# Interleaving the high and low activation halves, and moving four sums of squares from GpSimd to VectorE

## The reference

```python
def rmsnorm(x, g):                       # ahead of every layer
    return x * rsqrt(mean(x * x, axis=-1) + EPS) * g

x = x + rglru(rmsnorm(x, a_norm_g))      # norm 0
kv = rmsnorm(x, kv_norm_g) @ w_kv        # norm 1 (the attention layer uses the same root)
x = x + swa(rmsnorm(x, b_norm_g), kv)    # norm 1, second gain
x = x + 0.5 * swiglu(rms_norm(x, ffn1_norm))       # norm 2
x = x + hybrid_mixer(rms_norm(x, mix_norm))        # norm 3
x = x + 0.5 * swiglu(rms_norm(x, ffn2_norm))       # norm 4
return rms_norm(x, final_norm)                     # norm 5
# swiglu(x) = (silu(x @ w_gate) * (x @ w_up)) @ w_down, d_ff = 2816
```

## Time and profile before

| | us |
|---|---|
| Median of three runs (825.06 to 826.43) | 826.13 |
| The profiled execution | 825.43 |
| Its span, first to last instruction | 823.3 |
| TensorE busy | 799.1 |
| VectorE busy | 576.3 |
| ScalarE busy | 488.9 |
| GpSimd busy | 125.4 |

### The profile page before, as it was taken

How to read it: one execution, slowest core, us unless ns; L and a number is a source line. 1 busy time by engine, 2 the same in 40 slices (tenths; PEclk the granted TensorE clock), 3 DMA queues, 4 the chain that set the end, 5 groups by cost and what they waited for, 6 DMA issues and landing times.

```text
span 823.3 us, 15019 instructions
## 1 busy us (share of the span) xinstructions
PE 799.1 (97%) x5557; PEld 730.7 (89%) x5557; DVE 576.3 (70%) x840; ACT 488.9 (59%) x764; POOL 125.4 (15%) x172
## 2 busy tenths in 40 slices
PE   8999899799899999999999999999999999999997
PEld 7999899798699888889998889998999888888885
DVE  5987978777669787777448755466587788777443
ACT  7679855667756665555346455665747565555343
POOL 9305600325704000000003003000001200000000
PEclk9999999999999999999999999999999999999999
DMA  8624466443326676665655544444545576665661
GB/s 268 208 78 128 132 214 194 146 138 101 103 79 198 196 218 182 181 199 159 217 183 147 189 153 130 153 129 128 180 140 178 172 228 182 192 185 181 198 185 52
DMA packets 101046, 136.31 MB, mean 166 GB/s; under 512 B 5065, under 2 KB 86401, under 8 KB 100993
## 3 DMA queue, kind: packets, MB, share of 16 engines
q1 hardware_dynamic: 99232, 133.23, 52.4%
q0 software_dynamic: 1600, 2.28, 1.0%
q10 hardware_dynamic: 160, 0.07, 0.0%
HBM read 134.51 MB, written 1.05 MB: 165 GB/s over the span
## 4 chain that ended last, share of the span: by engine, by line
PE 73%; DVE 3%; ACT 2%; POOL 1%; issue 1%; ACTq 0%; DVEq 0%; POOLq 0%
PE bank L528 25%; PE bank L597 17%; PE bank L594 10%; PE bank L641 7%; PE bank L536 6%; PE bank L592 2%; PE bank L825 1%; PE bank L845 1%; DVE w_lo L1534 1%; ACT arena L1055 1%; POOL arena L474 1%; PE bank L838 1%; ACT w_hi L1055 1%; DVE arena L1856 1%; PE bank L1018 1%
## 5 line engine op out<-in xcount | busy, mean ns | idle before, releaser
L1534 DVE TENSOR_TENSOR w_lo<-stage,w_hi 128x1024 fp32r<-128x1024 f32 x249 | 318.3, 1285 | 149.2 <-ACT w_hi L1055 148.7
L528 PE MATMUL bank<-acts,w_hi 128*128 128x256 f32 (+1 forms) x1936 | 355.0, 285 | 5.4 <-DVE w_lo L1534 2.6
L1055 ACT ACTIVATE w_hi<-stage 128x1024 fp32r<-128x1024 f32 (+1 forms) x251 | 261.5, 1049 | 98.9 <-PE bank L528 53.2
L528 PEld LDWEIGHTS bank<-acts,w_hi 128*128 128x128 f32 x1936 | 302.4, 192 | 10.1 <-issue 6.0
L528 PE MATMUL bank<-acts,w_lo 128*128 128x256 f32 (+1 forms) x968 | 274.5, 284 | 0.0
L597 PE MATMUL bank<-acts,w_hi 128*128 128x512 f32 x616 | 217.5, 396 | 0.0
L594 PE MATMUL bank<-acts,w_lo 128*128 128x256 f32 x704 | 189.7, 280 | 0.0
L528 PEld LDWEIGHTS bank<-acts,w_lo 128*128 128x128 f32 x968 | 186.2, 192 | 0.0
L597 PEld LDWEIGHTS bank<-acts,w_hi 128*128 128x128 f32 x616 | 115.7, 188 | 25.5
L594 PEld LDWEIGHTS bank<-acts,w_lo 128*128 128x128 f32 x704 | 132.7, 188 | 3.6
L1055 ACT ACTIVATE arena<-bank 128x512 f32<-128x512 f32 (+1 forms) x79 | 44.1, 558 | 69.9 <-PE bank L597 46.5
(11 more groups left out here) (187 smaller groups left out, 711.0 us busy)
## 6 DMA issues: line engine op xcount, KB each, us to landing
stage<-ffn_w_gate SPq DMA_DIRECT2D x44, 512.0 KB, 4.2
stage<-ffn_w_up SPq DMA_DIRECT2D x44, 512.0 KB, 4.4
stage<-ffn_w_down SPq DMA_DIRECT2D x44, 512.0 KB, 4.0
stage<-w_in SPq DMA_DIRECT2D x40, 512.0 KB, 3.6
stage<-a_w_in SPq DMA_DIRECT2D x24, 512.0 KB, 4.7
stage<-b_w_in SPq DMA_DIRECT2D x16, 512.0 KB, 3.6
stage<-a_w_out SPq DMA_DIRECT2D x12, 512.0 KB, 4.0
stage<-b_w_out SPq DMA_DIRECT2D x8, 512.0 KB, 3.5
```

What stands on the lines that cost most here:

```text
L528: mm = pe.matmul(dst, w[:, slot, c:c + P], a[:, k, :] if isinstance(k, int) else wide(a[:, bass.ds(k, 1), :]), start=start and n == 0, sto ...
L1055: return nc.scalar.activation(out_, in_, func, **kw)
L1534: dve.tensor_tensor(w_lo[:, n % RING, 0:w], src, w_hi[:, n % RING, 0:w].bitcast(F32), ALU.subtract)\
```

## The change

The tensor `acts` gets another order: for each tile, high and low halves lie beside one another, so that `acts[:, k, :, :]` is one run of 512 columns, where before it was two runs of 256 that lie 30 tiles apart. Instructions that write several tiles of `a_hi` or `a_lo` at once now write runs of 256 with a gap of 256 between them, where before they wrote one run. No instruction is added or dropped for that.

All four calls of `square_sums` leave GpSimd's program. VectorE does the sums at the end of `norm`, in three instructions of 1024, 512 and 256 columns, each waiting for the one ahead of it.

```diff
+POOL_SUMS = []
+DVE_SUMS = [1, 2, 3, 4]
...
-        acts = sb("acts", [P, 2, 30, T], F32R)
-        a_hi, a_lo = acts[:, 0, :, :], acts[:, 1, :, :]
+        acts = sb("acts", [P, 30, 2, T], F32R)
+        a_hi, a_lo = acts[:, :, 0, :], acts[:, :, 1, :]
...
+        def each(t2):
+            return t2.rearrange("p (t n) -> p t n", n=T)
...
-            square_sums(1)
...
-            square_sums(2)
             pool.dma_start(fin_gain[:, :], I["final_norm_2"].rearrange("(o d) -> o d", o=1).to_broadcast([P, D]))\
                 .then_inc(fin_gain_in, 16)
-            square_sums(3)
             for h in range(NH):
                 normalise(NQ + h)
-            square_sums(4)
...
-                            pe.matmul(two[p][:, m, :], w_hi[:, half % RING, c:c + P], acts[:, :, k, :],
+                            pe.matmul(two[p][:, m, :], w_hi[:, half % RING, c:c + P], wide(acts[:, k, :, :]),
...
-                f(wide(a_hi[:, 8 + 2 * c:10 + 2 * c, :]), tiles(XB + 2 * c, 2), ACT.Copy).then_inc(xbh, 1)
+                f(a_hi[:, 8 + 2 * c:10 + 2 * c, :], each(tiles(XB + 2 * c, 2)), ACT.Copy).then_inc(xbh, 1)
...
-                return dve.tensor_tensor(dst_lo(dst, n), src, dst_hi(dst, n).bitcast(F32), ALU.subtract)
+                return dve.tensor_tensor(a_lo[:, dst:dst + n, :], each(src), a_hi[:, dst:dst + n, :].bitcast(F32), ALU.subtract)
...
                     if len(sets) > 1:
                         gained_lo(*sets[1], k)
+                if n in DVE_SUMS:
+                    i = 2 * DVE_SUMS.index(n)
+                    dve.wait_ge(sq_ready, 4 * n)
+                    dve.tensor_tensor(tiles(SQ, 4), tiles(SQ, 4), tiles(SQ + 4, 4), ALU.add).then_inc(sq_half, 1)
+                    dve.wait_ge(sq_half, i + 1)
+                    dve.tensor_tensor(tiles(SQ, 2), tiles(SQ, 2), tiles(SQ + 2, 2), ALU.add).then_inc(sq_half, 1)
+                    dve.wait_ge(sq_half, i + 2)
+                    dve.tensor_tensor(tiles(SQ), tiles(SQ), tiles(SQ + 1), ALU.add).then_inc(sq_sum, 1)
```

More of the change, by code:

```diff
@@ L242, in build @@
         v_raw, tok_raw = sem("v_raw"), sem("tok_raw")
-        sq_add, sq_sum = sem("sq_add"), sem("sq_sum")
+        sq_add, sq_sum, sq_half = sem("sq_add"), sem("sq_sum"), sem("sq_half")
         q_raw, hn_sq, hn_sum, hn_std, hn_tok, hn_turn, hn_done = (
@@ L477, in square_sums @@
                 pool.wait_ge(sq_ready, 4 * n)
+                done = 3 * POOL_SUMS.index(n)
                 plus(0, 2, 2)
                 plus(4, 6, 2)
-                pool.wait_ge(sq_add, 3 * n - 1)
+                pool.wait_ge(sq_add, done + 2)
                 plus(0, 4, 2)
-                pool.wait_ge(sq_add, 3 * n)
+                pool.wait_ge(sq_add, done + 3)
                 pool.tensor_tensor(tiles(SQ), tiles(SQ), tiles(SQ + 1), ALU.add).then_inc(sq_sum, 1)
-            square_sums(1)
             def normalise(n):
@@ L528, in passes @@
                     mm = pe.matmul(dst, w[:, slot, c:c + P],
-                                   a[:, k, :] if isinstance(k, int) else wide(a[:, bass.ds(k, 1), :]),
+                                   a[:, k, :] if isinstance(k, int) else a[:, bass.ds(k, 1), :],
                                    start=start and n == 0, stop=stop and n == 2, skip_group_check=True)
@@ L596, in wide_half @@
                         if k:
-                            mm = pe.matmul(two[p][:, m, :], w_hi[:, half % RING, c:c + P], acts[:, :, k, :],
+                            mm = pe.matmul(two[p][:, m, :], w_hi[:, half % RING, c:c + P], wide(acts[:, k, :, :]),
                                            start=False, stop=k == KD - 1, skip_group_check=True)
@@ L1226, in y_up @@
                 act.wait_ge(y_f, g + 1)
-                f(wide(a_hi[:, 8 + 3 * g:11 + 3 * g, :]), tiles(XB + 3 * g, 3), ACT.Copy).then_inc(y_hi, 1)
+                f(a_hi[:, 8 + 3 * g:11 + 3 * g, :], each(tiles(XB + 3 * g, 3)), ACT.Copy).then_inc(y_hi, 1)
             silu(0)
@@ L1317, in out_hi @@
                 act.wait_ge(yb_f, c + 1)
-                f(wide(a_hi[:, 8 + 2 * c:10 + 2 * c, :]), tiles(16 + 2 * c, 2), ACT.Copy).then_inc(yb_hi, 1)
+                f(a_hi[:, 8 + 2 * c:10 + 2 * c, :], each(tiles(16 + 2 * c, 2)), ACT.Copy).then_inc(yb_hi, 1)
             def gate_silu(c):
@@ L1379, in pair @@
                     act.wait_ge(ff_f, first + j + 1 + i * 2)
-                    f(wide(a_hi[:, bass.ds(i * 4 + (8 + 2 * j), 2), :]) if j >= 3 else wide(a_hi[:, 8 + 2 * j:10 + 2 * j, :]),
-                      tiles(44 + 2 * (j % 2), 2), ACT.Copy).then_inc(ff_hi, 1)
+                    f(a_hi[:, bass.ds(i * 4 + (8 + 2 * j), 2) if j >= 3 else slice(8 + 2 * j, 10 + 2 * j), :],
+                      each(tiles(44 + 2 * (j % 2), 2)), ACT.Copy).then_inc(ff_hi, 1)
                 for j in range(3):
@@ L1425, in branch_hi @@
                 act.wait_ge(o_done, NQ + 4 * b + 4)
-                f(wide(a_hi[:, 8 + 2 * b:10 + 2 * b, :]), bank[6 + b % 2][:, :], ACT.Copy).then_inc(ym_hi, 1)
+                f(a_hi[:, 8 + 2 * b:10 + 2 * b, :], each(bank[6 + b % 2][:, :]), ACT.Copy).then_inc(ym_hi, 1)
             H_M = half_of(C_MIX)
@@ L1486, in _ @@
                 act.wait_ge(mg_f, i + 1)
-                f(wide(a_hi[:, 16 + t:16 + t + n, :]), tiles(t, n), ACT.Copy).then_inc(mg_hi, 1)
+                f(a_hi[:, 16 + t:16 + t + n, :], each(tiles(t, n)), ACT.Copy).then_inc(mg_hi, 1)
                 if i == 2:
@@ L1984, in pair @@
                         at = bass.ds(i * 4 + (8 + 2 * j), 2)
-                        dve.tensor_tensor(wide(a_lo[:, at, :]), hid, wide(a_hi[:, at, :]).bitcast(F32), ALU.subtract)\
+                        dve.tensor_tensor(a_lo[:, at, :], each(hid), a_hi[:, at, :].bitcast(F32), ALU.subtract)\
                             .then_inc(ff_lo, 1)
```

## The result

The changed kernel takes 817.67 us (median of 5 runs, 817.54 to 817.85) against 826.33 us (median of 5 runs, 825.06 to 826.50): ratio 0.9899, 95% interval 0.9885 to 0.9912. The profiled execution took 817.76 us with a span of 816.0. Forecast were 818.2 us. The kernel before lay at 825.9 to 826.3 us from one group of runs to the next, so the 8.7 us here and the 8.1 us of the experiments are the same gain within their intervals.

A forecast was written before the change was run, and what follows sets the result against it. TensorE was taken to bound the kernel, busy 799.1 of 823.3 us. 825.43 - 5.75 (norm 1 with clock) - 1.0 (norm 3) - 1.2 (layout) = 817.5, plus 0.7 for the median: 818.2 us; 8-in-10 range 814.0 to 822.0.

The forecast's parts named there:

- The wait of norm 1: At norm 1, TensorE's wait for GpSimd's sum goes; its half starts 4.3 us earlier, with a new 0.6 us wait.
- The wait of norm 3: At norm 3, TensorE's wait ahead of the squares' matmuls goes: 1.0 us gained.
- Norms 2 and 4: TensorE never waited for these sums; VectorE's block fits, with 1.1 us of slack left at norm 2: 0 gained.
- The clock: Behind norm 1's wait TensorE runs at half clock; the clock staying up returns 1.45 us.
- The layout: In the FFN couples, contiguous operands save between nothing and 2.5 us; the middle, 1.2 us, was taken.
- Rival (a): In the FFN couples the layout gives nothing and the sums give all: 819.4 us; chance 0.27.
- The writes that now skip a tile: ScalarE's and VectorE's writes of 512 or 768 columns in two or three runs were costed at nothing.
- (c): At norm 1 the wait moves instead of going: 819.6 us, or 821.9 with a 3.5 us block; chance 0.12.
- (d): The attention stages, where TensorE waits for VectorE's maxima, take back 2 to 6 us: 820.2 to 824.2; chance 0.06.
- Rival (e): VectorE's block delays `w_lo` at all norms; gain 20.7 - 4x for x us, negative from 5.2: slower; chance 0.04.

The follow-up runs named there:

- the kernel with the doubled block: Changed kernel with each of VectorE's three addition sizes first run once more as a maximum that changes no value: 824.66 us, ratio 0.9986.
- The kernel with the filled wait: Kernel before, with TensorE filling most of its norm 1 wait for GpSimd with 18 small matmuls of ones: 823.66 us, ratio 0.9971.
- the layout alone: Changed kernel with the new layout kept and all four sums back on GpSimd: 825.99 us, ratio 1.0001.
- the sums alone: Changed kernel with the old layout back and all four sums on VectorE: 817.78 us, ratio 0.9904.
- the first four kernels: The first four experiment kernels, which shared their runs of the kernel before, at 825.88 us.
- the block behind the low half: Changed kernel, but at norm 1 the first of three low halves goes ahead of VectorE's block of additions: 818.22 us, ratio 0.9905.

## Why the prediction was right, and where it was not

**The wait of norm 1** was read rightly, and its pieces are within 0.3 us: block 2.40 us (forecast 2.4), squares' matmuls at 153.86 (153.9), half at 154.73 (155.0, the new wait being 0.37 instead of some 0.6). The half is earlier because VectorE began its block at 151.13 and not at 151.26, and because the first `w_lo` starts 0.08 us before the block's last addition ends, which pays for the two waits on itself (0.04 and 0.03 us).

**The wait of norm 3** went as forecast: the squares' matmuls start 7.1 us earlier than before, 1.0 more than the first FFN's end (6.1). **Norms 2 and 4** cost nothing; at norm 2 1.2 us of slack were left where 1.1 were forecast, and the kernel with the doubled block shows that the slack was real and finite.

**The clock** is the term that was too small: "returns 3.3 x (1 - 0.36/0.64) = 1.45 us". The kernel with the filled wait gives 2.5 us by medians (1.5 to 3.3). The term was right for the profiled execution, which was one of the quicker ones of the kernel before (825.43 where 21 runs have their median at 825.88). In another execution with the same wait, that of the layout alone, the clock fell already during the wait and stayed low for longer, as its windows show:

```profile
156.50:158.70 2.20, 0.00 (x0) 0.51 0.73 211
159.20:162.90 3.70, 3.70 (x18) 0.50 0.49 151
163.40:165.00 1.60, 1.60 (x16) 1.00 0.91 256
```

There the roots' matmuls start at 164.19, 2.0 us behind those of the filled wait, where the kernel before was 1.5 behind. What makes up the rest of the 2.5 us isn't shown; no execution with the whole of it was profiled.

**The layout** is the term that was too large: 1.2 us taken as the middle between 0 and 2.5, measured 0 within 0.1%. The step that failed is "Over 704 couples the difference of 3.6 ns is 2.5 us": the difference was real, but it was set against rows of uniform streams, and it is there in both layouts: 350.1 ns a couple before and 349.9 after by the starts. The rule that the prediction weighed against it, of the Trainium skill, "TensorE: Matmul & The Clock Gate", "Back-to-back issue gap", that a step depends on the number of columns alone, is borne out as far as runs of 256 columns go (the two windows with 487 and 443 matmuls each). It does not give the 3.6 ns: the same number of columns takes a step of 226.7 or of 233 ns here, by the stream it stands in. Rival (a) had the layout right, but its 819.4 us took over the small clock term. The writes that now skip a tile cost nothing, as taken: VectorE's 19 writes of 512 columns into `acts` take 687 ns each, where they took 688.

The sum shows how they met: forecast 5.75 + 1.0 + 1.2 = 7.95 us; in the profiles the waits give 159.34 - 154.73 = 4.6 and 1.0; with the clock's 2.5 by medians and the layout's 0 it is 8.1 in all, which is what the sums alone gave (825.88 - 817.78). The parts agree less well than the sum: put back alone, norm 1 cost 6.7 us, not 4.6 + 2.5 = 7.1, and the rest 1.5, not 1.0. And that the forecast came within 0.5 us is luck in part: a layout 1.2 us too large made up for a clock some 1 us too small. Rivals (c) and (d) are out: TensorE's clock stayed up behind the new wait, and its wait for VectorE's maxima in the attention stages is 3.2 us in three places, as before. Rival (e) needed a block of 5.2 us. At 4.8 us its formula foretold norm 1's start and norm 2's wait to 0.1 us, but it had norm 4's at 1.2 us for 0.6, and it left out that the clock falls again.

## What to carry to other kernels

When the engine that bounds a kernel waits at one fixed place, look at what stands there before changing what runs everywhere: four short sums, two of which were waited for, were 1% here, and a new layout under 704 matmul couples was nothing. Count such a wait twice, once for its length and once for the clock behind it, and take the second from several executions. Work that is moved to an in-order engine must be timed against what it pushes back: here 2.4 us fitted and 4.8 did not.

## What was not expected

**Most of the spread of the runs goes with the fall of the clock at norm 1.** The 21 runs of the kernel before that the first four kernels shared lie between 825.28 and 826.37, and the 11 with the doubled block between 823.16 and 826.20, 3.0 us apart. Kernels whose clock stays up at norm 1 in the profiled execution lie within 0.3 to 0.6 us: the changed one 817.54 to 817.85, the sums alone 817.44 to 817.98, the filled wait 823.51 to 823.86. The filled wait is the clearest case, since it still has the wait and only lacks the fall of the clock; its own runs of the kernel before lay between 825.32 and 826.96. The mean granted clock of a run does not order the times of the kernel before (0.993 at 825.6 to 826.1 us, 0.995 at 825.3 to 826.5): low clock inside the wait, as in the windows of the layout alone, lowers the mean while TensorE stands anyway.

**The clock falls in a second place, and not always.** At 97.8 to 101.0 us, behind the wait of 1.77 us in the recurrent layer, TensorE ran at 0.50 in the execution of the kernel before and at 0.61 in that of the changed one. In those of the sums alone, of norms 2 and 4 on GpSimd and of the block behind the low half it ran at 1.00, after the same wait. With the fall TensorE comes to norm 1 about 0.3 us later (the squares' matmuls at 153.86 against 153.52). Timelines of two kernels can differ by that much without an edit's having done it.

**GpSimd's additions slow VectorE by more than the additions cost on VectorE.** Three `w_lo` took 6.75 us beside them and 3.49 us without: 3.26 us, where VectorE's own block is 2.40. In this kernel VectorE's slack hid that at norms 2 and 4.
